# A hybrid decoder trunk on one core: high and low tokens as one moving operand, and retention outputs by token tile

## The reference

```python
def swiglu(x, w1, w3, w2):                       # layer 0: D_FF = 2816
    return (jax.nn.silu(x @ w1) * (x @ w3)) @ w2

# layer 1, retention: 4 heads, dk 256, dv 512, chunks of 128 tokens
    s = jnp.einsum('bhcd,bhmd->bhcm', qc, kc) * intra[None]
    o = jnp.einsum('bhcm,bhme->bhce', s, vc) \
        + jnp.einsum('bhcd,bhde->bhce', qc, R) * q_decay[None, :, :, None]
...
    o = o * lax.rsqrt(jnp.mean(o * o, axis=-1, keepdims=True) + RMS_EPS)
    o = o.reshape(B, T, H * dv).astype(h.dtype)
    return ((jax.nn.silu(g) * o) @ wo).astype(h.dtype)
```

## Time and profile before

| | us |
|---|---|
| median of 3 runs (lowest, highest) | 1709.44 (1709.34, 1713.52) |
| the profiled execution | 1709.88 |
| its span | 1708.1 |
| PE busy | 1617.9, 95% |
| DVE busy | 1227.7, 72% |
| ACT busy | 958.2, 56% |

### The profile page before, as it was taken

The page is one execution under the profiler, slowest core; times in us unless marked ns, Lnnn a source line. Parts: engine busy times, 40 slices in busy tenths (PEclk is TensorE's granted clock), DMA queues, the critical chain, the costliest instruction groups (busy, mean ns, idle before and its releaser), DMA issues.

```text
span 1708.1 us, 25921 instructions
## 1 busy us (share of the span) xinstructions
PE 1617.9 (95%) x10288; PEld 1357.8 (79%) x10288; DVE 1227.7 (72%) x938; ACT 958.2 (56%) x777; POOL 47.4 (3%) x26
## 2 busy tenths in 40 slices
PE   4999889899979997979999999999999999999997
PEld 3776875899869886768888888888888888888886
DVE  4565345455457444399889888898898898888896
ACT  2321222444343344277777777777777777777774
POOL 1000500000000000010000000000000000000100
PEclk8999999999999998989999999999999999999999
DMA  4446213555545452369999999999999999999992
GB/s 167 148 148 252 96 52 130 184 180 181 189 172 173 172 197 74 136 258 421 383 358 416 362 373 406 359 386 387 354 410 372 357 414 370 367 396 374 391 411 94
DMA packets 70180, 472.68 MB, mean 277 GB/s; under 512 B 7136, under 2 KB 7264, under 8 KB 17248
## 3 DMA queue, kind: packets, MB, share of 16 engines
q1 hardware_dynamic: 66080, 456.55, 69.3%
q10 hardware_dynamic: 2880, 10.91, 1.7%
...
## 4 chain that ended last, share of the span: by engine, by line
PE 92%; DVE 5%; ACT 1%; issue 1%; DMA 0%; DVEq 0%; ACTq 0%
PE ps L1290 90%; PE ps L1728 1%; DVE mem L992 1%; PE ps L1302 0%; DVE pairs_r L862 0%; DVE mem L886 0%; ACT workr L593 0%; PE ps L1720 0%; DMA h<-x 0%; PE ps L1638 0%; ACT work L577 0%; DVE work L1078 0%; DVE mem L978 0%; DVE h L870 0%; DVE work L842 0%
## 5 line engine op out<-in xcount | busy, mean ns | idle before, releaser
L1290 PE MATMUL ps<-pairs_r,workr 128*128 128x512 f32 x2856 | 659.5, 389 | 2.0 <-DVE workr L1084 2.0
L1290 PEld LDWEIGHTS ps<-pairs_r,workr 128*128 128x128 f32 x2856 | 535.3, 188 | 112.9 <-DVE workr L1084 2.2
L1290 PE MATMUL ps<-workr 128*128 128x512 f32 x2024 | 483.5, 393 | 2.8 <-DVE workr L1183 2.8
L1290 PEld LDWEIGHTS ps<-workr 128*128 128x128 f32 x2024 | 375.6, 188 | 80.0 <-issue 3.3
L1209 DVE TENSOR_TENSOR workr<-ring,workr 128x2048 fp32r<-128x2048 f32 x167 | 380.6, 2289 | 55.1 <-ACT workr L764 54.8
L1209 DVE TENSOR_TENSOR pairs_r<-ring,pairs_r 128x2048 fp32r<-128x2048 f32 x165 | 374.5, 2288 | 21.7 <-ACT pairs_r L764 19.5
L764 ACT ACTIVATE pairs_r<-ring 128x2048 fp32r<-128x2048 f32 x165 | 316.9, 1920 | 114.7 <-PE ps L1290 104.8
L764 ACT ACTIVATE workr<-ring 128x2048 fp32r<-128x2048 f32 x167 | 319.3, 1917 | 43.4 <-PE ps L1290 36.8
L1290 PE MATMUL ps<-mem 64*64 64x64 f32 (+8 forms) x3384 | 248.1, 263 | 28.2 <-DVE mem L886 11.1
L862 DVE TENSOR_TENSOR pairs_r<-ring,pairs_r 128x2048 fp32r<-128x2048 f32 x68 | 155.9, 2293 | 146.0 <-ACT pairs_r L601 144.8
L1290 PEld LDWEIGHTS ps<-mem 64*64 64x64 f32 (+5 forms) x3384 | 190.4, 151 | 84.7 <-issue 60.4
...
## 6 DMA issues: line engine op xcount, KB each, us to landing
...
```

The source lines that it names most:

```text
L1290: ins = nc.tensor.matmul(*args, **kw)
```

## The change

Two parts. In the dense mixer the high and low tokens lie side by side in one tile (`uT2`), k by k. The high weights meet both in one matmul of 512 columns, the low weights meet the high tokens in one of 256, so the w1 product has a bank for itself and the w3 product another: high tokens' sums in the left half, the product with the low tokens in the right. ACT copies the right halves out (`low2`), DVE adds the left halves (`both2`), and silu and product read from there. A unit uses two banks, in turn two pairs, and PE waits for DVE's sum of two units back. The high and low parts of a unit's result are made one unit later.

In the retention, output i is head i % 4 of token tile i // 4. ACT takes a root after four squares, and loads the table for it ahead of the first square. DVE gates tile 0, then stores the low parts of tile 0's first two groups, then gates tile 1. PE transposes tile 0, multiplies k = 0 to 3 of it, transposes tile 1, and goes on as the loops at the end of the diff say. Banks 4 and 5 hold tile 0 of the projection, 6 and 7 tile 1. Tile 0 is added to the residual first, and the last norm's first square waits for tile 0 alone.

The diff, cut to its core (of the retention's DVE and PE code the new lines only, the semaphores' names left out):

```diff
-    uTh, uTl = (wk(a, 2048, "k t", workr, k=KT) for a in (2048, 4096))
+    uT2 = wk(2048, 4096, "k x t", workr, k=KT, x=2)
+    uTh, uTl = uT2[:, :, 0, :], uT2[:, :, 1, :]
+    low2 = wk(18432, 1024, "b x t", b=2, x=2)
+    both2 = wk(19456, 1024, "b x t", b=2, x=2)
...
     rcount = {}
     for who in "ad":
         mine = [j for j in rjobs if j[2] == who]
+        if who == "d":
+            mine = mine[:3 * RH] + [("o", i) for i in range(4)] + [("t", 0), ("t", 1)]
+            mine += [("o", i) for i in range(4, 8)] + [("t", i) for i in range(2, 8)]
         rcount.update({j[:2]: n + 1 for n, j in enumerate(mine)})
     rstores_a = rcount[("g", 7)]
     rwho = {j[:2]: j[2] for j in rjobs}
...
+    def hidden_banks(f):
+        return ps[:, 2 * (f % 2):2 * (f % 2) + 2, :]
...
-                    a.wait_ge(s_h, 4 * n - (1 if n > 1 else 2) + (1 if n > 1 else 2) * t)
+                    a.wait_ge(s_h, 4 * n - (1 if n == 2 else 2) + (1 if n == 2 else 2) * t)
...
         split(2)
+        def ffn_high(f):
+            a.wait_ge(s_fa, f + 1)
+            act_f(hTh[:, f, :], a32[:, f % 2, :], ACT.Copy).then_inc(s_fah, 1)
         for f in range(FT):
             a.wait_ge(s_fh, f + 1)
             if f >= 2:
+                a.wait_ge(s_ft, f - 1)
+            act_f(low2[:, f % 2], hidden_banks(f)[:, :, T:2 * T], ACT.Copy).then_inc(s_fc, 1)
+            if f:
+                ffn_high(f - 1)
+            split(f + PAIRS)
+            a.wait_ge(s_ft, f + 1)
+            if f >= 2:
                 a.wait_ge(s_fa, f - 1)
-            act_f(sl[:, f % 2, :], ps[:, f % 4, 0:T], ACT.Silu).then_inc(s_fs, 1)
-            split(f + PAIRS)
-            a.wait_ge(s_fa, f + 1)
-            act_f(hTh[:, f, :], a32[:, f % 2, :], ACT.Copy).then_inc(s_fah, 1)
+            act_f(sl[:, f % 2, :], both2[:, f % 2, 0, :], ACT.Silu).then_inc(s_fs, 1)
+        ffn_high(FT - 1)
         for i in range(U_W2 + PAIRS, U_Q + PAIRS - 1):
             split(i)
...
             if kind == "o":
+                if i == 0:
+                    a.preload_act_table(ACT.Sqrt)
                 a.wait_ge(s_rj, rnum[j[:2]] + 1)
                 if i >= 1:
                     a.wait_ge(s_oss, i)
                 act_f(osq, bank, ACT.Square, accum_out=rss[:, i:i + 1]).then_inc(s_oss, 1)
-                if i == 7:
-                    a.wait_ge(s_om, 1)
-                    act_f(rsd, rss, ACT.Sqrt).then_inc(s_or, 1)
+                if i % 4 == 3:
+                    a.wait_ge(s_om, i // 4 + 1)
+                    act_f(rsd[:, i - 3:i + 1], rss[:, i - 3:i + 1], ACT.Sqrt).then_inc(s_or, 1)
             elif kind in "vg":
                 if i % 2 == 0:
                     u0 = (U_V if kind == "v" else U_G) + i
...
-        def add_to_h(n, order=(0, 1, 2, 3)):
+        def add_to_h(n, order=(0, 1, 2, 3), banks=(4, 5, 6, 7)):
-                V.tensor_tensor(dst, dst, ps[:, 4 + q, :], ALU.add).then_inc(s_h, 1)
+                V.tensor_tensor(dst, dst, ps[:, banks[q], :], ALU.add).then_inc(s_h, 1)
...
-        for f in range(FT):
-            v.wait_ge(s_fs, f + 1)
-            if f >= 2:
-                v.wait_ge(s_fal, f - 1)
-            V.tensor_tensor(a32[:, f % 2, :], sl[:, f % 2, :], ps[:, f % 4, T:2 * T], ALU.mult).then_inc(s_fa, 1)
-            split(f + PAIRS)
+        def ffn_low(f):
             v.wait_ge(s_fah, f + 1)
             V.tensor_tensor(hTl[:, f, :], a32[:, f % 2, :], hTh[:, f, :].bitcast(F32),
                             ALU.subtract).then_inc(s_fal, 1)
+        for f in range(FT):
+            v.wait_ge(s_fc, f + 1)
+            if f >= 2:
+                v.wait_ge(s_fa, f - 1)
+            V.tensor_tensor(both2[:, f % 2], low2[:, f % 2], hidden_banks(f)[:, :, 0:T], ALU.add).then_inc(s_ft, 1)
+            if f:
+                ffn_low(f - 1)
+            split(f + PAIRS)
+            v.wait_ge(s_fs, f + 1)
+            V.tensor_tensor(a32[:, f % 2, :], sl[:, f % 2, :], both2[:, f % 2, 1, :], ALU.mult).then_inc(s_fa, 1)
+        ffn_low(FT - 1)
         for i in range(U_W2 + PAIRS, U_Q + PAIRS - 1):
             split(i)
         add_to_h(1)
...
+        def mean_square(t):
+            v.wait_ge(s_oss, 4 * t + 4)
+            z = rss[:, 4 * t:4 * t + 4]
+            V.tensor_scalar(z, z, 1.0 / RV, EPS, ALU.mult, ALU.add).then_inc(s_om, 1)
+        def root(t):
+            v.wait_ge(s_om, t + 1)
+            v.wait_ge(s_or, t + 1)
+            rsqrt(rss[:, 4 * t:4 * t + 4], rsd[:, 4 * t:4 * t + 4], rrs[:, 4 * t:4 * t + 4])
+        def gate_o(i):
+            t, hd = i // 4, i % 4
+            dst = og[:, t, hd * RV:(hd + 1) * RV]
+            V.scalar_tensor_tensor(out=dst, in0=ps[:, rnum["o", i] % 8, :], scalar=rsd[:, i:i + 1], in1=dst,
+                                   op0=ALU.mult, op1=ALU.mult).then_inc(s_rd, 1)
+        def gated_low(i):
+            t, kg = i // 4, i % 4
+            to = slice(t * P, (t + 1) * P)
+            v.wait_ge(s_rA, rstores_a + i + 1)
+            V.tensor_tensor(ogTl[:, 4 * kg:4 * kg + 4, to],
+                            ps[:, rnum["t", i] % 8, :].rearrange("p (k s) -> p k s", k=4),
+                            ogTh[:, 4 * kg:4 * kg + 4, to].bitcast(F32), ALU.subtract).then_inc(s_rd, 1)
+        mean_square(0)
+        root(0)
+        v.wait_ge(*rstored(("g", 7)))
+        for i in range(4):
+            gate_o(i)
+        mean_square(1)
+        gated_low(0)
+        gated_low(1)
+        root(1)
+        for i in range(4, 8):
+            gate_o(i)
+        for i in range(2, 8):
+            gated_low(i)
+        add_to_h(2, (0, 2, 1, 3), (4, 6, 5, 7))
...
             w = split_unit(f, "k g n", k=KT, g=2)
-            if f >= 4:
-                pe.wait_ge(s_fa, f - 3)
+            if f >= 2:
+                pe.wait_ge(s_ft, f - 1)
             for i in range(2):
                 for k in range(KT):
-                    ins = M3(ps[:, f % 4, i * T:(i + 1) * T], parts(w, k, i), parts(uT_, k),
-                             start=(k == 0), stop=(k == KT - 1))
+                    bank = hidden_banks(f)[:, i, :]
+                    M(bank, w[0][:, k, i, :], uT2[:, k, :, :].rearrange("p x t -> p (x t)"), start=(k == 0),
+                      stop=False, skip_group_check=True)
+                    ins = M(bank[:, 0:T], w[1][:, k, i, :], uTh[:, k, :], start=False, stop=(k == KT - 1),
+                            skip_group_check=True)
             ins.then_inc(s_fh, 1)
             owed.append(s_pu)
         for f in range(FT):
...
-                hd, t = i // 2, i % 2
+                t, hd = i // 4, i % 4
...
                         ins = M(bank[:, cs], ST[:, hd, 256:384], vtok[:, 1, vs], start=False, stop=True)
+            if ins is not None:
+                ins.then_inc(s_rj, 1)
+        def turn_gated(t):
+            for kg in range(4):
+                pe.wait_ge(*rstored(("o", 4 * t + kg)))
                 for q in range(4):
                     k = 4 * kg + q
+                    ins = nc.tensor.transpose(ps[:, rnum["t", 4 * t + kg] % 8, q * P:(q + 1) * P],
+                                              og[:, t, k * P:(k + 1) * P], ident)
                 ins.then_inc(s_rj, 1)
+        def retention_output(k, t):
+            w = split_unit(U_O + k // 2, "g n", g=2)
+            if k % 4 == 0:
+                pe.wait_ge(*rstored(("t", 4 * t + k // 4)))
+            if k == 0:
+                pe.wait_ge(*rstored(("t", 2 * t + 1)))
+            for c in range(2):
+                ins = M3(ps[:, 4 + 2 * t + c, :], parts((ogTh, ogTl), k, slice(t * P, (t + 1) * P)),
                          parts(w, k % 2, slice(c * 512, (c + 1) * 512)),
                          start=(k == 0), stop=(k == 15), skip_group_check=True)
                 if k == 15:
                     ins.then_inc(s_acc, 1)
+            if t and k == 15:
                 owed.append(s_pu)
+            elif t and k % 2:
                 ins.then_inc(s_pu, 1)
+        turn_gated(0)
+        for k in range(4):
+            retention_output(k, 0)
+        turn_gated(1)
+        for k in (4, 5):
+            retention_output(k, 0)
+        for k in range(6):
+            retention_output(k, 1)
+        for k in range(6, 14):
+            for t in range(TT):
+                retention_output(k, t)
+        for t in range(TT):
+            for k in (14, 15):
+                retention_output(k, t)
         pe.wait_ge(s_gd4, 1)
```

40 lines of the change are left out of this document (6 added, 34 removed).

## The result

| us | before | after |
|---|---|---|
| median (lowest, highest) of 6 runs each, one comparison | 1714.63 (1709.34, 1718.74) | 1700.45 (1699.45, 1701.55) |
| profiled execution | 1709.88 | 1699.45 |
| its span | 1708.1 | 1697.6 |

The ratio is 0.9921, with a 95% interval of 0.9900 to 0.9942: faster by more than the 0.3% that can be told. The forecast step was 1696.3/1709.44 = 0.9923. In microseconds the time came 4.2 over the forecast, 0.05 inside the upper edge of its range. Three further comparisons had before at medians of 1713.82, 1713.01 and 1713.34 (19, 17 and 17 runs), and a fourth at 1709.79 (one run, beside e9 to e12). So the 1709.44 of three runs, on which the number was built, stood some 4 us under the level of this kernel.

The account below looks back on a forecast made before the run. The prediction took PE, busy 95% of the span, as the bound. Its terms 4.5 + 8.6 + 0.2 = 13.3 us off 1709.88 gave 1696.6, stated as 1696.3 against the runs' median 1709.44; range 1692.5 to 1700.5.

Parts of the forecast that it names:

- Part A: Dense mixer's hidden stage: one matmul instruction in three goes, 12.7 ns less a triple, 4.5 us off.
- the 13 ns: Hidden stage: each matmul carries 13.3 to 14.0 ns beside its columns, whatever its width.
- Both rows give the same fixed part: Hidden stage: reason for taking 4.5 us, from 120.0 ns at 256 columns and 227.3 ns at 512.
- Rival 3: Hidden stage: weight load paces the 256-column matmul, so gain there is 0 or 1 us; 1700.6 or 1698.9; chance 13%.
- Part B: Retention outputs by token tile: outputs' end to projection's end falls from 60.46 to 50.1 us, 10.3 off.
- Rival 5: Retention end: gap stays, DVE does tile 1's root and gates before lowering tile 0; 1700 us; chance 2%.
- The clock behind PE's gap: Retention projection: granted clock falls after PE idles 2.1 us, 1.75 us back, net 8.6 off.
- the main case: Whole kernel: clock falls behind the retention gap, 13.3 us off in all, 1696.3 us; chance 40%.
- rival 1: Retention end: clock stays at its full level, same sum without the 1.75, 1694.6 us; chance 30%.
- GpSimd next to DVE: Retention end: DVE's gates not held by GpSimd's product, cost 0; bound 1.9 us if they stand still.
- The hand-over: Projection to last norm: tile 0's additions and square lie under tile 1's matmuls; 2.37 becomes 2.15 us, 0.2 off.
- What is saved ahead of it should come out whole: Expert layer: unbroken PE work, untouched and waiting for no date, so earlier savings reach the total undiminished.

Follow-up runs that it names:

- e9: Changed kernel with the high weights' product issued as two 256-column matmuls instead of one of 512; 1704.14 us (one run).
- e12: Changed kernel with the shorter filler matmuls on constants in two norms, run again for its profile; 1694.55 us (one run).
- e10: Changed kernel with the low weights' 256-column matmul cut into two of 128 columns; 1737.73 us (one run).
- e5: Kernel before with the shorter filler matmuls on constants in two norms; median 1708.94 us, ratio 0.9977.
- e6: Kernel before with the retention's part of the change alone, plus the shorter filler matmuls in two norms; median 1700.21 us, ratio 0.9917.
- e2: Kernel before with the retention's part of the change alone; median 1700.46 us, ratio 0.9919.
- e7: Changed kernel with the shorter filler matmuls on constants in two norms; median 1695.21 us, ratio 0.9891.
- e3: The changed kernel run again, on the same chip as its two halves; median 1698.80 us, ratio 0.9918.
- e4: Changed kernel with longer, oversized filler matmuls on constants in two norms; 1708.26 us (7 runs).
- e8: Changed kernel with shorter filler, and tile 0's first two high copies and low parts ahead of second root and mean square; 1693.60 us, ratio 0.9884.
- e15: Changed kernel, no filler, with tile 0's first two high copies and low parts ahead of second root and mean square; 1697.13 us, ratio 0.9907.
- e16: Changed kernel without the early load of the root's table; 1700.05 us (one run).

## Why the prediction was right or wrong

**Part A, 4.5 us.** What was counted was right: the number of matmuls decides (e9), 5.55 us a unit for 5.56 forecast, DVE 0.81 us ahead. Whether the 13 ns are a fixed part or the load's is open. The size is 4.67 in the short rhythm and 2.34 in the long, and the forecast knew no second rhythm. That the profile after has the short one is luck. In that profile the stretch gave 3.45 and not 4.67, since its first unit ran longer at the lower clock than before's. "Both rows give the same fixed part" was good enough for 256 and 512 columns and no law: at 128 it fails by 48 ns (e10). Rival 3 (part A comes to 0 or 1) did not come; the long rhythm goes halfway to it.

**Part B, 10.3 us before the clock.** Measured 10.63 in the profile, and 8.7 (medians) or 10.3 (ratios) between e5 and e6. The chain of small steps came out within 0.25 us (4.26 for 4.5), the two hand-overs without a gap, and the fourth weight unit in time. Rival 5 did not come.

**The clock behind PE's gap, 1.75 back.** The profile after has none, but it was a fair price and a poor date. Of twelve profiles with part B, five have the fall. Here e2, chain of waits:

```profile
666.52 7.31 PE ps L1321 x24
```

7.31 instead of 5.71 for these 24 matmuls, 1.6 us (e2, e6, e7, e10, e12; not in after, e3, e4, e8, e9, e15, e16). Weighted so, the cost was 0.7 us, and the choice between the main case and rival 1 was an even one. One reading behind it was short: "it stayed at 1.00" after the second norm is true of 509.50 to 513, but the clock had been at 0.50 from 503 to 507 and had only just risen.

**GpSimd next to DVE, 0.** Right. Four gates took 2.73 us, whether GpSimd's product ran beside them (after: from 659.28) or not (after: from 664.17). The small op on SBUF alone was held until GpSimd's end each time: 0.49 us to 661.21 in after, 0.83 to 661.84 in e16, where GpSimd ended at 661.18 and 661.82; and 0.16 in e15, where it comes after that end. Only that hold, some 0.3 us, was on the path, and e15 takes it off together with the rest of the order's 1.25. The rule of the Trainium skill ("GPSIMD Engine Reference", section "1. Specifications") that was quoted agrees with both: the op was held, the gates with one SBUF input were not. In which mode the held op runs no trace here shows.

**The hand-over, 0.2.** Measured 0.36: the square was there 0.15 sooner than counted.

**The step that failed** lies in the sum: it has no term for the code that is not changed, and it starts from three runs. "What is saved ahead of it should come out whole" was argued for the expert layer, and there it held (986.71 and 986.62 us from the last norm's mean square on). For the 308.78 us ahead of the dense mixer and the 138.48 ahead of the retention outputs the same was taken without a reason, and there the two profiles differ by 2.63 and 1.40, 4.0 us, where the sum has 0. What the runs show is that the clock falls at different times in them: the time of before follows its own mean clock, from 1709.03 us at 0.982 to 1718.46 at 0.975, and two of the three runs that the number started from (1709.34 and 1709.44) were at the low end of that.

For the profiled execution the sum then reads: 13.3 us forecast, 10.4 measured. Part A with its first unit gave 1.0 less than its 4.5, part B with the clock 2.0 more than its 8.6, the hand-over 0.2 more, and the unchanged code took 4.0. The forecast step of 13.1 us is met by the ratio (13.5 of 1709.44, or 14.2 of the medians), but its interval runs from 10 to 17 us, so that this is no proof of the terms and partly luck. The absolute time was missed by 4.2, about what the reference was low. (The working's own 13.3 from 1709.44 gives 1696.1 and not 1696.3.) A range of 8 us did not have room for this: with the spread of a single kernel (1709 to 1719 before, 1693 to 1705 after) it should have been some 12.

**What stays open.** What picks the rhythm of the pairs, why the clock falls in one execution behind a given gap and not in the next, and whether part A makes it fall more. Whether the filler also acts by another way than the clock was not tried.
